# One block of programs for the two expert layers, and each token's two experts taken in order of their number

## The reference, cut to what matters

```python
_, idx = lax.top_k(jnp.where(in_group, biased, -jnp.inf), TOP_K)     # two experts of one group
w = jnp.take_along_axis(s, idx, axis=-1)
w = w / jnp.sum(w, axis=-1, keepdims=True)
for e in range(N_EXPERTS):
    hid = silu(flat @ w_gate[e]) * (flat @ w_up[e])
    out = out + combine[:, e:e + 1] * (hid @ w_down[e])
x = x + g2 * out
```

## Time and profile before

| | |
|---|---|
| median of three runs | 1167.51 us (1164.26 to 1169.11) |
| profiled execution | 1164.08 us, its span 1162.2 us |
| mean granted TensorE clock | 0.964 |
| busy: TensorE, VectorE, ScalarE, GpSimd | 1037.1, 928.3, 608.6, 140.4 us |
| read and written | 308.72 MB and 23.15 MB, 286 GB/s over the span |

### The profile page before, as it was taken

How to read it: one execution, slowest core, us unless ns; L and a number is a source line. 1 busy time by engine, 2 the same in 40 slices (tenths; PEclk the granted TensorE clock), 3 DMA queues, 4 the chain that set the end, 5 groups by cost and what they waited for, 6 DMA issues and landing times. The chain is left out here.

```text
span 1162.2 us, 13900 instructions
## 1 busy us (share of the span) xinstructions
PE 1037.1 (89%) x4832; PEld 790.4 (68%) x4832; DVE 928.3 (80%) x1043; ACT 608.6 (52%) x614; POOL 140.4 (12%) x172
## 2 busy tenths in 40 slices
PE   6889999998898995999999999928689999999990
PEld 1466767776565444788888888827568888888870
DVE  4578888976894325699999999856659999999975
ACT  1534222213565104477777777533357777777841
POOL 0100200000110000520000000041242100000005
PEclk9899999998999998999999999969899999999995
DMA  9715878676023003999999999967299999999956
GB/s 370 270 59 216 290 257 300 241 271 263 10 73 127 27 37 109 250 413 413 414 413 414 414 413 413 348 236 291 70 264 400 413 414 415 413 414 414 412 227 235
DMA packets 145981, 332.44 MB, mean 286 GB/s; under 512 B 14096, under 2 KB 16088, under 8 KB 145808
## 3 DMA queue, kind: packets, MB, share of 16 engines
q1 hardware_dynamic: 125768, 277.99, 63.4%
q10 hardware_dynamic: 12680, 28.68, 6.6%
q0 software_dynamic: 7488, 25.19, 5.8%
HBM read 308.72 MB, written 23.15 MB: 286 GB/s over the span
## 5 line engine op out<-in xcount | busy, mean ns | idle before, releaser
L1886 DVE TENSOR_TENSOR w_lo<-ring,w_hi 128x2048 fp32r<-128x2048 f32 x192 | 432.5, 2285 | 32.5 <-ACT w_hi L1726 29.2
L1726 ACT CAST w_hi<-ring 128x2048 fp32r<-128x2048 f32 x192 | 364.8, 1914 | 142.9 <-DMA ring<-in_moe_w_up 57.9
L1992 PE MATMUL bank<-w_hi,xT_hi 128*128 128x512 f32 x512 | 203.4, 397 | 7.4 <-DVE xT_lo L1893 6.0
L1992 PE MATMUL bank<-w_hi,xT_lo 128*128 128x512 f32 x512 | 199.9, 390 | 0.0
L1992 PE MATMUL bank<-w_lo,xT_hi 128*128 128x512 f32 x512 | 199.4, 389 | 0.0
L1399 PE MATMUL bank<-ring_last_parts,arena_parts 128*128 128x512 f32 (+1 forms) x320 | 116.7, 395 | 5.0 <-DVE ring_parts L1016 2.7
L1992 PEld LDWEIGHTS bank<-w_hi,xT_hi 128*128 128x128 f32 x512 | 96.1, 188 | 28.9 <-DVE xT_lo L1893 7.7
L1992 PEld LDWEIGHTS bank<-w_hi,xT_lo 128*128 128x128 f32 x512 | 96.2, 188 | 20.8
L1074 DVE SCALAR_TENSOR_TENSOR gate_b<-ring,silu_c,gate_b 128x512 f32<-128x512 f32 x140 | 105.9, 756 | 4.5
L1992 PEld LDWEIGHTS bank<-w_lo,xT_hi 128*128 128x128 f32 x512 | 96.3, 188 | 19.1
L1399 PE MATMUL bank<-ring_parts,arena_parts 128*128 128x512 f32 (+1 forms) x256 | 99.7, 389 | 0.0
(11 more groups left out here) (261 smaller groups left out, 1440.4 us busy)
## 6 DMA issues: line engine op xcount, KB each, us to landing
ring<-in_moe_w_gate SPq DMA_DIRECT2D x64, 1024.0 KB, 12.4
ring<-in_moe_w_up SPq DMA_DIRECT2D x64, 1024.0 KB, 13.4
ring<-in_moe_w_down SPq DMA_DIRECT2D x64, 1024.0 KB, 11.9
ring<-in_ada_w SPq DMA_DIRECT2D x21, 2048.0 KB, 8.7
y_scratch<-shared ACTq DMA_DIRECT2D x30, 512.0 KB, 6.7
ring<-in_w_in ACTq DMA_DIRECT2D x21, 512.0 KB, 3.8
shared<-in_ada_w SPq DMA_DIRECT2D x2, 2048.0 KB, 16.0
x_res<-in_x SPq DMA_DIRECT2D x8, 512.0 KB, 12.4
```

The lines of the kernel that those rows point to most:

```text
L1726: nc.scalar.copy(w_hi[:, buf(u, p), :], half(raw(e, p))).then_inc(s_hi, 3 if isinstance(e, int) and (e, p) == (-1, 3) else 1)
L1886: V.tensor_tensor(w_lo[:, buf(u, p), :], half(raw(e, p)), w_hi[:, buf(u, p), :].bitcast(F32), ALU.subtract).then_inc(s_lo, 3 if isinstance ...
L1992: last = pe.matmul(bank[:, b, :], xs[:, kk, :], ws[:, k, :], start=(kk == 0 and i == 0), stop=(kk == KD - 1 and i == 2))
```

## The change

1. The five blocks after the first front become one. `moe(l, front)`, `pooling` and `last_norm` now return a program per engine, and a single block calls them one after the other on each engine. `stage_over` between them goes. Where a barrier used to order things, a wait on a semaphore stands: POOL waits for the four stores of `xhat` before layer 1's first gather, each engine waits for the count before reading it, and POOL waits for the last stores (`rows_stored`) after reading the count.
2. The two experts of a token are ordered by number. Choice 0 is the lower, so its row never belongs to expert 15.
3. The rows of choice 0 are gathered by POOL as soon as expert 14's rows are stored (and expert 15's up product no longer needs the ring's middle slot, to which they go), and VectorE adds all four tiles of them before it adds any of choice 1. `Combine.fetch` gathers only choice 1.
4. `pool_scale` and `final_norm_w` are loaded at the end of the experts' program on SyncE's queue, into `next_row`, instead of at the start of the stage that uses them.

```diff
+                link(ins)
+                for c, pick_of in ((0, ALU.min), (1, ALU.max)):
+                    ins = V.tensor_tensor(e_sel[:, c, :], e_raw[:, 0, :], e_raw[:, 1, :], pick_of)
                 link(ins)
...
                 V.tensor_copy(idx[:], bank[:, 4, NT * NE:NT * NE + 3]).then_inc(s_idx, 1)
+                V.tensor_scalar(row_early[:], row_tmp[:, 0, 0, :], float(LAST * P - 1), None, ALU.min
+                                ).then_inc(s_early, 1)
...
+                pool.wait_ge(s_early, 1)
+                pool.wait_ge(s_lo, pos_count(NE - 2, 3))
+                pool.wait_ge(s_yst[0], 16 * (NE // 2 + 1))
+                pool.wait_ge(s_yst[1], 16 * (NE // 2))
+                for t in range(NT):
+                    pool.indirect_dma_start(
+                        out=first_rows[:, t, :], out_offset=None, in_=y_dram[0:LAST * P, :],
+                        in_offset=bass.IndirectOffsetOnAxis(ap=row_early[:, t:t + 1], axis=0)).then_inc(early[t], 16)
...
+            def over_gpsimd(pool, combine):
+                pool.wait_ge(s_cnt, 1)
+                most = pool.value_load(max_count[0:1, 0:1])
+                rows_stored(pool)
+                with pool.If(most > P):
...
+                    combine.fetch_first_again(pool)
+                    combine.fetch(pool, LIST_N)
+                with pool.Else():
+                    combine.fetch(pool, NE * P)
...
+            def add_first(self, dve):
+                for t in range(NT):
+                    dve.wait_ge(early[t], 16 * (self.l + 1))
+                    self.add_one(dve, 0, t, self.chain)
...
+            def fin_vector(dve):
+                combine.add_first(dve)
                 combine.add(dve, 0)
                 combine.add(dve, 1)
-                dve.wait_ge(f_ld, 16)
+                dve.wait_ge(mixture.s_pool, 16)
...
+            @block.vector
+            def _(dve):
+                moe0.vector(dve)
+                moe0.over_vector(dve, combine0)
+                pool_vector(dve)
+                moe1.vector(dve)
+                moe1.over_vector(dve, combine1)
+                fin_vector(dve)
```

More of the change, by code:

```diff
@@ L15 @@
+from collections import namedtuple
 from contextlib import ExitStack
@@ L118, in build_program @@
         half_load = [nc.alloc_semaphore(name=f"half_slot{r}_loaded") for r in range(6)]
+        early = [nc.alloc_semaphore(name=f"first_choice_rows_loaded{t}") for t in range(NT)]
         held = []
@@ L1989, in product @@
                         for k in range(n):
                             kk = (p % 2) * n + k
-                            for i, (xs, ws) in enumerate(((xT_hi[:, xb], hi), (xT_hi[:, xb], lo), (xT_lo, hi))):
-                                last = pe.matmul(bank[:, b, :], xs[:, kk, :], ws[:, k, :], start=(kk == 0 and i == 0),
-                                                 stop=(kk == KD - 1 and i == 2))
-                        last.then_inc(s_used, 3 if isinstance(e, int) and (e, p) == (-1, 3) else 1)
@@ L2064, in _ @@
-                    for e in range(NE - 3, LAST):
-                        step(e, e % 2, 16 * ((e + 2) // 2 + 1) if e + 2 < NE else None)
-                    down_last()
-            stage_over()
+                keep_busy(16)
+                rows_T(0, 16)
+                keep_busy(5)
+                pe.wait_ge(s_xlo, 1)
+                product(2, -1, 0, 0, 0)
+                product(2, -1, 0, 1, 0)
+                rows_T(1, 16)
+                product(3, -1, 0, 2, 0)
+                product(3, -1, 0, 3, 0)
@@ L2217, in build_program @@
-        moe(0)
-        stage_memory(33500)
-        normw_ffn, at = carve(14000, D)
-        front1 = Front(1, normw_ffn)
-        assert front1.at.end <= 14000
-        rows, at = carve(at, 2, NT, D)
-        combine = Combine("combine0", rows)
-        pool_w, at = carve(at, len(WINDOWS), 2, 2 * P)
-        xhat, at = carve(at, NT, D)
-        pooledT, at = carve(at, KD, SEQ)
-        pool_scale = pooledT[:, 0:2, :].rearrange("p k t -> p (k t)")
-        assert at <= 33500
-        scale_c, shift_c, normw_c = (pool_cols[:, i * KD:(i + 1) * KD] for i in range(3))
@@ L2241, in build_program, with over_sync @@
-        with nc.Block() as block:
-            @block.sync
-            def _(sp):
-                sp.dma_start(pool_scale, a["pool_scale"][0].partition_broadcast(P)).then_inc(p_ps, 16)
+            def over_sync(sp):
+                sp.wait_ge(s_cnt, 1)
+                most = sp.value_load(max_count[0:1, 0:1])
+                with sp.If(most > P):
+                    rows_stored(sp)
+                    for t in range(NT):
+                        sp.wait_ge(early[t], 16 * (l + 1))
+                    for e, b, n in blocks(sp):
+                        sp.wait_ge(v_d, n + 1)
+                        put(sp, wg, e, 0, KD).then_inc(v_ld, 16)
+                        put(sp, wu, e, 1, KD).then_inc(v_ld, 16)
+                        put(sp, wd, e, 2, KE).then_inc(v_ld, 16)
+                    sp.wait_ge(v_st, 16 * MORE * NE)
@@ new lines, in pooling, with pool_sync @@
+        def pooling(mixture):
+            stage_memory(33500)
+            normw_ffn, at = carve(14000, D)
+            front1 = Front(1, normw_ffn)
+            assert front1.at.end <= 14000
+            rows, at = carve(at, NT, D)
+            combine = Combine(0, rows)
+            pool_w, at = carve(at, len(WINDOWS), 2, 2 * P)
+            xhat, at = carve(at, NT, D)
+            pooledT, at = carve(at, KD, SEQ)
+            assert at <= 33500
+            scale_c, shift_c, normw_c = (pool_cols[:, i * KD:(i + 1) * KD] for i in range(3))
+            band_sum = pool_cols[:, 3 * KD:3 * KD + 1]
+            p_ = lambda s: sem(f"pool_{s}")
+            p_sq, p_rs, p_xh, p_pl = p_("square_sum"), p_("rstd"), p_("xhat"), p_("pooled")
+            p_ea, p_ed = p_("pooled_copied_by_act"), p_("pooled_copied_by_dve")
+            p_mx, p_xr, p_dc, p_pc = p_("mixed"), p_("x_updated"), p_("dve_chain"), p_("pool_chain")
+            p_wg, p_cs = p_("weights_gated"), p_("columns_ready")
+            K_ORDER = (0, 1, 4, 5, 2, 3, 6, 7)
+            BY_ACT, BY_DVE = K_ORDER[0::2], K_ORDER[1::2]
+            def pool_sync(sp):
```

1020 lines of the change are left out of this document (516 added, 504 removed).

## The result

The changed kernel is slower: median 1172.39 us (1166.71 to 1177.3, 20 runs) against 1165.65 (1162.74 to 1169.11, 20 runs), ratio 1.0058, 95% interval 1.0048 to 1.0069. The forecast was 1157.5, worked out from the median of the three runs known then, 1167.51; from the 1165.65 of twenty it would have been 1155.7. The changed kernel's profiled execution took 1173.02 us, span 1171.1, clock 0.967.

The account below looks back on a forecast made before the run. It took the loops as full on TensorE and DMA, with only the seams movable. Gains 5.3 + 3.8 + 1.45 less 0.56 added work made 10.0 us, so 1167.51 became 1157.5, range 1150 to 1163.

Parts of the forecast that it names:

- The step that failed: Loops over the experts: TensorE and DMA engines busy all of the time, body untouched, so both passes keep their length.
- Rival 1: Seams between expert loops and following stages: the advance is kept whole, 15.8 us less, 1151.7 us; chance 0.15.
- the seams: Stretches where TensorE stands still: layer 0's experts to pooling mixer, mixer to layer 1's experts, layer 1's experts to end.
- Rival 2: Both expert seams: early gathers delay the last stores, so second gathers start no earlier; gain 5 us, 1162.5; chance 0.11.
- Rival 3: Expert loops: moved code refetches instructions each pass, up to 2.3 us per pass, 27.6 in all, 1185 us; chance 0.06.
- Layer 0's seam and the routing: Layer 0's experts to layer 1's: 3.8 us gained before pooling, 1.45 from barriers before routing, less 0.28 added work.
- the first scaling: Pooling mixer, token tile 0: the first scaling ends at 773.9 instead of 777.5 us, a gain of 3.6.
- POOL's first root: Layer 0's seam, tile 0: root beside VectorE's additions, taken as 2.1 us with the instruction ahead of it.
- The end: Layer 1's last rows to the last output multiplication: 21.3 us instead of 26.6, a gain of 5.3 (bounds 3.8 to 6.9).
- The added work: Routing of each layer: two 128x4 min and max instructions with one link, costing 0.28 us per layer, 0.56 in both.
- the 0.5% line of the prediction: Whole kernel: 0.5% of the median, 5.8 us, taken as what a measurement can tell from no change.

Follow-up runs that it names:

- b1: The kernel before with an unused 64-byte tensor ahead of max_count, shifting ring and shared region to byte 42816: 1177.01 us, ratio to before 1.0094.
- a1: The changed kernel with row_early packed beside max_count in one 32-byte tensor, so the ring starts at its old byte 42752: 1159.13 us, ratio to before 0.9945.
- d2: a1 with next_row loaded right after the first four halves of each layer's expert weights instead of behind the last: 1158.25 us, ratio to before 0.9941.
- e1: The changed kernel with row_early declared behind the ring and next_row loaded after the first four halves of weights: 1158.56 us, ratio to before 0.9950.
- c1: The kernel before with bias_cols, silu_c and mod (256 bytes) declared behind the ring, which then starts at byte 42496: 1163.74 us, ratio 1.0000.
- c2: The kernel before with bias_cols alone (64 bytes) declared behind the ring, which then starts at byte 42688: 1176.72 us, ratio 1.0106.
- c3: The kernel before with a 64-byte pad between ring and shared; the ring stays at 42752, shared and arena move: 1164.76 us, ratio 1.0006.
- f1: The kernel before with a 32-byte pad ahead of max_count, so the ring starts at byte 42784: 1181.62 us, ratio 1.0144.
- f2: The kernel before with rstd (32 bytes) declared behind the ring, which then starts at byte 42720: 1178.00 us, ratio 1.0105.
- b2: The kernel before with an unused 128-byte tensor ahead of max_count, so the ring starts at byte 42880: 1178.24 us, ratio to before 1.0095.
- d1: a1 with the four early gathers issued only after the count is read and the last stores have landed: 1164.57 us, ratio to before 0.9994.

## Why the prediction was wrong

**The step that failed** is the first: "nothing in the change touches that loop's body, so its two passes should keep their length". The body is not touched, but the address to which its weights go is. The runs put 399 GB/s in the place of 414, 18.4 us per expert in the place of 17.7, 13.5 us in both loops; b1, which has only the shift, shows the same 13.1 (585.09 against 571.95). What misled me was the reading of the earlier trace rows: TensorE and the DMA engines both at full share. Seven MB per expert over the rate gives the period exactly, so the transfers bound the loop: with q1's packets 3.2% longer in the mean (96.5 to 99.6 ns) the period grew by 3.8% (17.73 to 18.41 us). I had counted instructions and queues, and no addresses. The difference of the medians says the same: 1172.39 - 1159.13 = 13.3 us between the changed kernel and a1.

**Rival 1**, the advance kept whole, did not come: the seams gave 9.1 of its 15.8. **Rival 2** was half right. The second gathers start 5.60 and 5.71 us after the last rows of the two layers, where the first gather of before started 5.93 and 5.73: 0.3 earlier in layer 0 and no earlier in layer 1, though they are four instead of eight. But the last stores don't hold them: in layer 1 POOL's queue is past its wait for them and branches on the count at 1145.39, and the gathers start at 1148.72, behind the four early ones that began late.

**Rival 3** put a loss in the loops, by a mechanism that no run shows: no instruction queue moved anything between 540 and 720 us, and a1 has the same single block with loops of before's length.

**Layer 0's seam and the routing** were forecast at 3.8 + 1.45 - 0.28 = 4.97 and gave 4.89 (a1 4.52, d2 4.36, e1 5.13): 3.47 at the first pooling matmul, 0.16 from there to the scores, 1.49 for the barriers, less 0.23 from the routing to the first product. Of the 3.8, 3.6 was the first scaling; the 0.2 beyond it was an estimate of mine, for which the runs show 64 pooling matmuls in 9.80 us instead of 9.98. The first pooling matmul came 16.87 us after the last rows, forecast 16.7, but that agreement is luck. The early gathers began 3.77 us after the store's issue, at the late edge of the forecast's 2.6 to 3.8, and one of them took 1.78 instead of 0.94. VectorE, itself ready 0.7 later than forecast, then waited 1.06 for their rows, so the early additions ended 12.0 after the last rows instead of 10.3 and tile 0 was complete at 13.3 instead of 12.1. Against that POOL's first root, forecast at 2.1 with the instruction ahead of it, took 0.84 (781.44 to 782.28). The 1.2 late and the 1.3 early cancel. TensorE's clock was granted at 0.50 until 787 us and at 1.00 from 788, after 17.60 us without a matmul; before it was 0.50 until 781 and 0.83 in the microsecond behind, after 21.06.

**The end** was forecast at 21.3 from the last rows and took 22.43, a gain of 4.2 instead of 5.3. The mis-sized term is the start of the early gathers, 4.73 after the store's issue instead of 2.6. The store took 3.9 to land, beside a fetch that the sum did not have, and POOL needs 0.8 more from there to the gather. A later error gave 0.9 back: the second gathers start 0.30 after the fourth early one and not 1.21. So they start 5.71 after the last rows and not 4.3, and tile 0 gets its second row at 11.65 instead of 10.2. The early additions were hidden only just: VectorE waited 5.07 and 1.17 for the early rows and ended 0.16 ahead of tile 0's second one, where the forecast had 1.6. With a quicker store, in d2, the end is at 21.71.

**The added work** is right: two instructions of 0.158 and a link, 0.27 per layer (forecast 0.28).

**Not in the sum**: 1.4 us between the last multiplication and the span's end. All six kernels with one block show it (5.7 from the start of that multiplication), the eight with separate blocks don't (4.3). In the trace it is POOL's DRAIN: 6.08 us in each of the six, 1.33 in each of the eight, from 0.63 us ahead of the last multiplication; SyncE, which waits for the output to land, is through 1.4 before it. Why the DRAIN is longer was not tried. Nor is the 3.07 before the first product explained: that stretch is 470.7 to 474.8 in before, b1, c1, c2, c3, f1 and f2, 478.6 in b2, 471.7 to 475.3 in five kernels with one block and 479.3 in d1, a scatter of single executions that is larger than it.

So of the forecast's 10.0 the order of work gives 6.4 by a1's ratio: the right sign and the right places, less 1.4 at the very end, 1.6 behind layer 1's last rows (3.7 for 5.3) and 0.5 in layer 0's seam. By the 0.5% line of the prediction that would have been just "faster", with an interval that reaches to the other side of the line (0.9924 to 0.9967); the place of the ring turned it into 0.58% slower.

## What to carry to other kernels

Where DMA engines are busy all of the time, work out bytes over rate; if that is the period, they are the bound however busy TensorE looks (here 7.34 MB at 414 GB/s, 17.7 us, with TensorE's share at 100%), and a change's declarations belong to its cost. Put a buffer that takes the bulk of such traffic at a multiple of 256 bytes (here 414 GB/s instead of 398 to 400) and keep small tensors behind it. When a profile after differs in a stretch that the change doesn't touch, compare GB/s at equal DMA share, then addresses, and try a pad on the old kernel.

## What the runs showed of the hardware that I had not expected

- A start of the weights' buffer off a multiple of 256 bytes costs 3.6% of the DMA rate (414 to 399 GB/s), the same at remainders of 32 to 224; packets go from exactly 84 and 159 ns to 87.5 and 164 in the mean. Gathers to a good place are slowed with them (c2: 161.4 instead of 159), and with the engines' share under 0.95 the median stays at 84.
- Reading the count and branching cost POOL nothing here, because its queue ran ahead: in after the read starts at 1144.97 and the branch is taken at 1145.39, beside the second early gather, and the gather behind the branch starts 0.30 after the fourth one ends, as without a branch. Between two blocks, with no gather in flight, the same read and branch had 1.21 ahead of the gather.
- The 16 KB instruction fetch near layer 1's store of expert 14 was one packet of 0.9 to 1.5 us in all fourteen traces, and where it ended after the 0.5 MB store's issue the store landed 2.1 to 2.2 us after the fetch's end (3.0 to 4.4 us after its issue, with 2.6 to 2.7 in the eight kernels with a block per stage).
- POOL's DRAIN at the end of the block took 6.08 us in the six kernels with one block and 1.33 in the eight with a block per stage, and it ended the span.
